# Sample attention of a decoder step: fp32 products replaced by three passes over high and low parts

## The chip, the cores and the metric

The kernel runs on one core of one Trainium2 chip. The metric is the device time of one execution in microseconds (us); lower is better. All times below come from the runs and from one profiled execution of the kernel before.

## The reference

One inference step of a small decoder: a gated convolution layer, a projection to shared keys and values, dilated window attention of 2048 prompt tokens, and the same for 8 samples with one new token each, whose older keys and values lie in a cache. The part around the change is the samples' attention. For each of three head groups (`GROUPS`), each of 8 samples and each of 2 key/value heads, 4 query heads attend to 128 cached keys and to the new one:

```python
def window_attn_sample(q, kc, vc, n_past, window, dilation):
    ...
    s = jnp.einsum('btkgd,btnkd->btkgn', qg, kg) * SCALE
    lse = jax.nn.logsumexp(s, axis=-1)
    p = jnp.exp(s - lse[..., None])
    o = jnp.einsum('btkgn,btnkd->btkgd', p, vg).reshape(Bd, T, HEADS, HEAD_DIM)
    return o, lse.reshape(Bd, T, HEADS)
```

The three groups are then mixed with weights from their softmax denominators. Everything is fp32.

## The kernel before

The program is five phases, one after the other, with a barrier between them: convolution projection (names `a_`), convolution output (`b_`), prompt attention with its projections (`g_`), sample attention (`s_`, `sample_attention_phase`), and the output phase (`d_`). In phases a, b, g and d every large fp32 product is written as three passes: ScalarE (ACT) copies the operand into a tile of type fp32r (the high part), VectorE (DVE) subtracts it from the original (the low part), and TensorE (PE) accumulates high x high, high x low and low x high in PSUM.

The sample phase keeps plain fp32 products. Its engines run orders written out by hand; there is no scheduler, and semaphores alone tie the engines together.

- SyncE (SP) loads six half caches (`s_cache`, two per group), the queries and the new rows, and then the 16 row blocks of the two weight matrices of the output phase, through `RAW` buffers `w_raw`. Block k is issued when the low part of block k - RAW is made.
- TensorE turns the queries (`single("q", g)`), then for each group (`scores(g)`) turns the cached keys in quads of four 128x128 tiles (`turn_keys`, L1625) into two PSUM tiles `tps`, and multiplies each turned key tile with the 4 query columns that belong to it (L1644). A quad is turned while the one before it is still being worked on. Sixteen such products fill one PSUM bank; it is copied, turned back, goes through the softmax, and the probabilities are turned again. `values(g)` multiplies the 16 cached value tiles, straight from `s_cache`, with 4 columns of probabilities each (L1663). The order is: scores 0, scores 1, values 0, scores 2, values 1, values 2.
- ScalarE copies turned keys to SBUF (L1710), copies scores, does the exponentials, and in between makes the high parts of the weight blocks for the output phase (L1703).
- VectorE does the new key's scores, the maxima, the low parts of the weight blocks (L1781, L1784) and the final merge.

In all, L1644 and L1663 each stand for 48 products of a 128x128 stationary tile with 4 moving columns.

Of the kernel before, what the change touches and what calls it, by code (L numbers as in the profile page):

```python
# [14 lines left out]
F32 = mybir.dt.float32  # L15
F32R = mybir.dt.float32r
BF16 = mybir.dt.bfloat16
ALU = mybir.AluOpType
# [1477 lines left out]
def sample_attention_phase(nc, q_sample, new_rows, caches, o_sample, w_z, w_out, pre_gain, w_hi, w_lo):  # L1496
# [10 lines left out]
    with ExitStack() as ctx:  # L1507
        def sb(name, shape, dt=F32):
            return ctx.enter_context(nc.sbuf_tensor(f"s_{name}", shape, dt))
# [8 lines left out]
        cache = [sb(f"cache{c}", [P, NS // 2, 2 * KVW]) for c in range(2 * GROUPS)]  # L1518
        q_rows = sb("q_rows", [R, GROUPS, HD])
        new = sb("new", [R, GROUPS, 2, HD])  # L1520
        qt = [sb(f"qt{g}", [P, R]) for g in each]
        keys_t = [sb(f"keys_t{b}", [P, 4, P]) for b in range(2)]
        score_t = [sb(f"score_t{g}", [P, R]) for g in each]
        score = [sb(f"score{g}", [R, KEYS + 1]) for g in each]
        prob = [sb(f"prob{g}", [R, KEYS + 1]) for g in each]
        prob_t = [sb(f"prob_t{g}", [P, R]) for g in each]
        sum_t = [sb(f"sum_t{g}", [P, R]) for g in each]
        product = sb("product", [R, HD])
        sums = sb("sums", [R, GROUPS, HD])
        stat = sb("stat", [R, 4, GROUPS])  # L1530
        small = sb("small", [R, 4])
        merged = sb("merged", [R, HD])
        ident = sb("ident", [P, P])
        gains = sb("gains", [P, KT])
        RAW = 3
        w_raw = [sb(f"w_raw{b}", [P, D]) for b in range(RAW)]

        tps = [ps(f"tps{b}", [P, 4, P]) for b in range(2)]
# [6 lines left out]
        s_new_rows = sem("new_rows_landed")  # L1545
        s_cache = [sem(f"cache_landed{c}") for c in range(2 * GROUPS)]
        s_keys = sem("keys_turned")
        s_keys_sb = sem("keys_copied")
        s_one = sem("single_turned")
        s_one_sb = sem("single_copied")  # L1550
        s_st = sem("scores_t_ready")
# [57 lines left out]
        @block.tensor  # L1609
        def _(pe):  # L1610
            def single(kind, g, src, rows):

                n = SINGLES.index((kind, g))
                if n >= 2:
                    pe.wait_ge(s_one_sb, n - 1)
                nc.tensor.transpose(one[n % 2][0:src.shape[1], 0:rows], src, ident[0:rows, 0:rows]).then_inc(s_one, 1)

            def turn_keys(g, quad):

                n, c = 4 * g + quad, 2 * g + quad // 2  # L1620
                pe.wait_ge(s_cache[c], 16)
                if n >= 2:
                    pe.wait_ge(s_keys_sb, n - 1)
                for x in range(4):
                    t = nc.tensor.transpose(tps[n % 2][:, x, :],  # L1625
                                            cache[c][:, 2 * (quad % 2) + x // 2, (x % 2) * HD:(x % 2 + 1) * HD],
                                            ident[:])
                t.then_inc(s_keys, 1)

            def scores(g):  # L1630

                turn_keys(g, 0)
                for quad in range(4):
                    n = 4 * g + quad
                    if quad < 3:
                        turn_keys(g, quad + 1)
                    pe.wait_ge(s_keys_sb, n + 1)
                    if quad == 0:
                        pe.wait_ge(s_one_sb, done("q", g))
                        if g >= 2:  # L1640
                            pe.wait_ge(s_st_sb, g - 1)
                    for x in range(4):
                        row = (4 * quad + x) * QPK
                        t = nc.tensor.matmul(st_ps[g % 2][:, row:row + QPK], keys_t[n % 2][:, x, :],  # L1644
                                             qt[g][:, row:row + QPK], start=True, stop=True)
                t.then_inc(s_st, 1)

            def turn_scores(g):
                pe.wait_ge(s_st_sb, g + 1)
                single("score", g, score_t[g][:], P)  # L1650

            def turn_probs(g):
                pe.wait_ge(s_exp, g + 1)
                single("prob", g, prob[g][:, 0:KEYS], R)

            def values(g):

                pe.wait_ge(s_one_sb, done("prob", g))
                if g >= 2:
                    pe.wait_ge(s_ot_sb, g - 1)  # L1660
                for pair in range(NS * KVH):
                    seq, n = pair // KVH, pair % KVH
                    t = nc.tensor.matmul(ot_ps[g % 2][:, pair * QPK:(pair + 1) * QPK],  # L1663
                                         cache[2 * g + seq // 4][:, seq % 4, KVW + n * HD:KVW + (n + 1) * HD],
                                         prob_t[g][:, pair * QPK:(pair + 1) * QPK], start=True, stop=True)
                t.then_inc(s_ot, 1)

            def turn_sums(g):
                pe.wait_ge(s_ot_sb, g + 1)
                single("sum", g, sum_t[g][:], P)  # L1670

            pe.wait_ge(s_ident, 2)
            pe.wait_ge(s_q, 16 * GROUPS)
            for g in each:
                single("q", g, q_rows[:, g, :], R)
            scores(0)
            turn_scores(0)
            scores(1)
            turn_scores(1)
            turn_probs(0)  # L1680
            values(0)
            scores(2)
            turn_scores(2)
            turn_probs(1)
            turn_sums(0)
            values(1)
            turn_probs(2)
            values(2)
            turn_sums(1)
            turn_sums(2)  # L1690

        @block.scalar
        def _(act):
            def copy_single(kind, g, dst):
                act.wait_ge(s_one, done(kind, g))
                act.wait_ge(s_one_sb, done(kind, g) - 1)
                nc.scalar.activation(dst, bank(kind, g)[0:dst.shape[0], 0:dst.shape[1]], ACT.Copy)\
                  .then_inc(s_one_sb, 1)

            def split_weights(ks):  # L1700
                for k in ks:
                    act.wait_ge(s_wraw[k % RAW], 16 * (k // RAW + 1))
                    nc.scalar.activation(w_hi[:, k // KT, k % KT, :], w_raw[k % RAW][:], ACT.Copy,  # L1703
                                         scale=gains[:, k:k + 1] if k < KT else 1.0).then_inc(s_whi, 1)

            def keys(g, weights=()):
                for quad in range(4):
                    n = 4 * g + quad
                    act.wait_ge(s_keys, n + 1)
                    nc.scalar.activation(keys_t[n % 2][:], tps[n % 2][:], ACT.Copy).then_inc(s_keys_sb, 1)  # L1710
                    split_weights(weights[quad:quad + 1])
                act.wait_ge(s_st, g + 1)
                nc.scalar.activation(score_t[g][:], st_ps[g % 2][:, 0:R], ACT.Copy).then_inc(s_st_sb, 1)
                copy_single("score", g, score[g][:, 0:KEYS])

            def exponentials(g):
                act.wait_ge(s_bias, 2 * g + 2)
                nc.scalar.activation(prob[g][:], score[g][:], ACT.Exp, bias=stat[:, 0, g:g + 1], scale=SCALE,
                                     accum_out=stat[:, 1, g:g + 1]).then_inc(s_exp, 1)
                copy_single("prob", g, prob_t[g][:])  # L1720

            def copy_sums(g):
                act.wait_ge(s_ot, g + 1)
                nc.scalar.activation(sum_t[g][:], ot_ps[g % 2][:, 0:R], ACT.Copy).then_inc(s_ot_sb, 1)

            act.dma_start(gains[:], pre_gain.rearrange("(k p) -> p k", p=P),
                          allow_slow_non_contiguous=True).then_inc(s_gains, 16)
            for g in each:
                copy_single("q", g, qt[g][:])
            keys(0)  # L1730
            act.wait_ge(s_gains, 16)
            keys(1, range(0, 4))
            exponentials(0)
            split_weights(range(4, 6))
            copy_sums(0)
            keys(2, range(6, 10))
            exponentials(1)
            split_weights(range(10, 13))
            copy_sums(1)
            exponentials(2)  # L1740
            split_weights(range(13, 16))
            copy_sums(2)
            act.wait_ge(s_step, 3)
            nc.scalar.activation(stat[:, 2, :], stat[:, 3, :], ACT.Exp).then_inc(s_w, 1)

        @block.vector
        def _(dve):
            def new_score(g):

                if g > 0:  # L1750
# [24 lines left out]
            def split_weights(ks):  # L1775

                for k in ks:
# [5 lines left out]
                    else:  # L1783
                        nc.vector.tensor_tensor(lo, w_raw[k % RAW][:], hi, ALU.subtract).then_inc(s_wlo, 1)  # L1784

            dve.wait_ge(s_q, 16 * GROUPS)
            dve.wait_ge(s_new_rows, 16 * GROUPS)
            for g in each:
                new_score(g)
            maximum(0)  # L1790
            dve.wait_ge(s_gains, 16)
            split_weights(range(0, 4))
            maximum(1)
            split_weights(range(4, 10))
            maximum(2)
            add_new_value(0)
            split_weights(range(10, 16))

            least, total, inverse = small[:, 1:2], small[:, 2:3], small[:, 3:4]
            dve.wait_ge(s_bias, 2 * GROUPS)  # L1800
# [482 lines left out]
```

## Time and profile before

| What | Value |
|---|---|
| Time, median of 3 runs (lowest to highest) | 2868.02 us (2867.28 to 2869.19) |
| Span of the profiled execution, first to last instruction | 2864.1 us |
| What lies around the span, by the median | 3.9 us |
| PE busy / PE weight load busy | 2717.9 us (95%) / 2351.9 us (82%) |
| DVE busy / ACT busy | 1189.8 us (42%) / 973.7 us (34%) |
| Sample phase, first instruction to the first one of the output phase | 2361.33 to 2434.63 us: 73.3 us |

The profile gives no execution time of its own for the profiled run beside the span, so the 3.9 us is the median less the span. Each core instruction has a start and a length; a TensorE product shows as a weight load (PEld) and a matmul (PE), whose end is modelled, so the spacing of starts is the better measure of its cost. The granted TensorE clock is given as a share of 2.4 GHz: 1.00 is 2.4 GHz, 0.50 is 1.2 GHz.

### The profile page before, as it was taken

The numbers are of one execution on the slowest core, as the hardware profiler recorded it, in microseconds if no ns is written. First come the engines' busy times: TensorE is split into PE (matmuls) and PEld (weight loads), VectorE is DVE, ScalarE is ACT, GpSimd is POOL, SyncE is SP. The second block draws the span as 40 slices with busy tenths as digits, with TensorE's granted clock in tenths as the row PEclk, the third lists the DMA queues.
The fourth block names the chain that finished last, engine by engine and source line by source line (L and its number), as shares of the span: only waits on it lengthen the run. The fifth ranks groups of instructions, "written<-read, shape, count | busy, mean of one in ns | idle before, by whom it ended". The sixth has DMA issues, their size and how long they took to land. (4 is left out here: it accounts for less than half of the span.)

```text
span 2864.1 us, 39445 instructions
## 1 busy us (share of the span) xinstructions
PE 2717.9 (95%) x14124; PEld 2351.9 (82%) x14124; DVE 1189.8 (42%) x2209; ACT 973.7 (34%) x2163; POOL 449.0 (16%) x330
## 2 busy tenths in 40 slices
PE   6999999999799799999989999989999987899997
PEld 5999999999777568888858888877888867788884
DVE  7311111111243355555564554554444433455552
ACT  6211111111155434444443443343333333233332
POOL 1010110101012211111111111111111110233331
PEclk9999999999999999999999999999999985999999
DMA  4232323322455431111131111131111116433330
GB/s 155 85 103 70 109 95 106 103 70 95 142 189 174 139 130 49 41 40 41 63 104 43 48 48 41 46 120 51 60 59 59 50 37 210 170 133 133 134 119 31
DMA packets 128411, 264.49 MB, mean 92 GB/s; under 512 B 14125, under 2 KB 81541, under 8 KB 126794
## 3 DMA queue, kind: packets, MB, share of 16 engines
q1 hardware_dynamic: 122138, 219.41, 23.3%
q10 hardware_dynamic: 6192, 44.01, 4.8%
q8 instruction: 50, 0.82, 0.1%
q14 instruction: 31, 0.25, 0.0%
HBM read 198.21 MB, written 109.19 MB: 107 GB/s over the span
## 5 line engine op out<-in xcount | busy, mean ns | idle before, releaser
L1070 PE MATMUL g_proj<-g_w_hi,g_ht_hi 128*128 128x512 f32 (+1 forms) x1224 | 509.2, 416 | 19.7 <-DVE g_w_lo L1385 19.4
L1072 PE MATMUL g_proj<-g_w_hi,g_ht_lo 128*128 128x512 f32 (+1 forms) x1224 | 485.5, 397 | 0.0
L1071 PE MATMUL g_proj<-g_w_lo,g_ht_hi 128*128 128x512 f32 (+1 forms) x1224 | 485.1, 396 | 0.0
L249 PE MATMUL a_pair<-a_ht_hi,a_w_hi 128*128 128x412 f32 (+1 forms) x1280 | 448.9, 351 | 2.0 <-DVE a_ht_lo L409 2.0
L251 PE MATMUL a_pair<-a_ht_hi,a_w_lo 128*128 128x412 f32 (+1 forms) x1280 | 448.1, 350 | 0.0
L250 PE MATMUL a_pair<-a_ht_lo,a_w_hi 128*128 128x412 f32 (+1 forms) x1280 | 448.0, 350 | 0.0
L1070 PEld LDWEIGHTS g_proj<-g_w_hi,g_ht_hi 128*128 128x128 f32 (+1 forms) x1224 | 223.5, 183 | 72.9 <-DVE g_w_lo L1385 14.2
L1072 PEld LDWEIGHTS g_proj<-g_w_hi,g_ht_lo 128*128 128x128 f32 (+1 forms) x1224 | 223.1, 182 | 64.1 <-issue 3.2
L1071 PEld LDWEIGHTS g_proj<-g_w_lo,g_ht_hi 128*128 128x128 f32 (+1 forms) x1224 | 224.1, 183 | 49.5 <-issue 2.4
L249 PEld LDWEIGHTS a_pair<-a_ht_hi,a_w_hi 128*128 128x128 f32 x1280 | 241.6, 189 | 3.0 <-DVE a_ht_lo L409 2.4
L250 PEld LDWEIGHTS a_pair<-a_ht_lo,a_w_hi 128*128 128x128 f32 x1280 | 241.4, 189 | 1.0
L251 PEld LDWEIGHTS a_pair<-a_ht_hi,a_w_lo 128*128 128x128 f32 x1280 | 241.3, 188 | 0.6
L1456 POOL TENSOR_TENSOR g_q_rot<-g_rot_a,g_rot_b 128x512 f32<-128x512 f32 (+1 forms) x102 | 131.0, 1286 | 652.4 <-DVE g_rot_b L1355 652.4
L1258 ACT ACTIVATE g_probs<-g_score,g_part 128x256 f32<-128x256 f32 (+1 forms) x384 | 159.6, 428 | 114.5 <-DVE g_part L1379 114.5
L1371 DVE TENSOR_TENSOR g_score<-g_score,g_mask 128x1024 f32<-128x1024 f32 (+1 forms) x96 | 96.8, 1009 | 227.8 <-PE g_score L1103 227.8
L209 POOL TENSOR_TENSOR a_w_lo<-a_w_raw,a_w_hi 128x1024 fp32r<-128x1024 f32 x32 | 76.2, 2406 | 619.5 <-ACT a_w_hi L307 619.5
L1330 DVE TENSOR_TENSOR g_pt_lo<-g_tps,g_pt_hi 128x512 fp32r<-128x512 f32 x152 | 99.8, 687 | 119.5 <-ACT g_pt_hi L1228 119.5
L463 DVE TENSOR_TENSOR a_y<-a_pair,a_conved 128x412 f32<-128x412 f32 (+1 forms) x40 | 23.4, 586 | 293.7 <-ACT a_silu_z L329 293.7
L620 PE MATMUL b_out<-b_w_hi,b_y_hi 128*128 128x512 f32 (+1 forms) x272 | 108.2, 398 | 25.5 <-DVE b_w_lo L706 16.3
L1266 ACT ACTIVATE g_sum_t<-g_out 128x512 f32<-128x512 f32 x96 | 57.4, 598 | 204.2 <-PE g_out L1132 204.2
L427 DVE TENSOR_TENSOR a_u<-a_c,a_pair 128x412 f32<-128x412 f32 (+1 forms) x40 | 23.3, 583 | 232.7 <-ACT a_c L311 232.7
L329 ACT ACTIVATE a_silu_z<-a_pair 128x412 f32<-128x412 f32 (+1 forms) x40 | 20.6, 514 | 288.0 <-PE a_pair L251 288.0
(222 smaller groups left out, 4924.6 us busy)
## 6 DMA issues: line engine op xcount, KB each, us to landing
out_cache_kv_g_sample<-cache_kv_g ACTq DMA_DIRECT2D x72, 410.0 KB, 3.5
scratch_partial<-g_part SPq DMA_DIRECT2D x48, 520.0 KB, 2.9
d_part<-scratch_partial SPq DMA_DIRECT2D x48, 520.0 KB, 4.6
g_tok<-scratch_hn_rows SPq DMA_DIRECT2D x48, 512.0 KB
a_w_raw<-a_w_in SPq DMA_DIRECT2D x32, 512.0 KB, 5.4
a_x<-x_prompt SPq DMA_DIRECT2D x16, 512.0 KB, 3.5
b_y_raw<-scratch_y_t SPq DMA_DIRECT2D x16, 512.0 KB, 4.3
b_x<-x_prompt SPq DMA_DIRECT2D x16, 512.0 KB
```

What stands on the lines that cost most here:

```text
L209: nc.gpsimd.tensor_tensor(w_lo[k][:], w_raw[k % 2][:], w_hi[k][:].bitcast(F32), ALU.subtract).then_inc(s_wlo, 1)
L249: nc.tensor.matmul(out, hi, ht_hi[:, k, cols], start=(k == 0), stop=False)
L250: nc.tensor.matmul(out, hi, ht_lo[:, k, cols], start=False, stop=False)
L251: last = nc.tensor.matmul(out, lo, ht_hi[:, k, cols], start=False, stop=(k == KT - 1))
L620: nc.tensor.matmul(out, hi, w_hi[:, k, cols], start=(k == 0), stop=False)
L1070: nc.tensor.matmul(out, hi, w_hi[:, k, cols], start=(k == 0), stop=False)
L1071: nc.tensor.matmul(out, hi, w_lo[:, k, cols], start=False, stop=False)
L1072: last = nc.tensor.matmul(out, lo, w_hi[:, k, cols], start=False, stop=(k == KT - 1))
L1258: nc.scalar.activation(probs[:, h, cols], score[:, h, cols], ACT.Exp, bias=part[w.u % 2][:, D + x:D + x + 1], scale=SCALE, accum_out=part[ ...
L1330: nc.vector.tensor_tensor(lo, bank_view(at[1], width, hi), hi.bitcast(F32), ALU.subtract).then_inc(s_tr_free, 1)
L1371: nc.vector.tensor_tensor(score[:, :, cols], score[:, :, cols], m.unsqueeze(1).to_broadcast([P, QPK, width]), ALU.add).then_inc(s_masked, 1)
L1456: nc.gpsimd.tensor_tensor(dst[0:n, 0:heads * HD], rot_a[0:n, bank, 0:heads * HD], rot_b[0:n, bank, 0:heads * HD], ALU.add).then_inc(s_rot, 1)
```

## The change

The sample phase gets the three passes too. Turned queries, turned keys, cached values and turned probabilities are each split into a high part (ACT, fp32r) and a low part (DVE), and each fp32 product becomes three accumulating fp32r products. The values, which were used straight from the cache, are now first split into `v_hi` and `v_lo`, one pair of buffers per half cache, used again for each group. The single turned tiles of queries and probabilities are released by DVE's subtraction in place of ACT's copy. In the same diff the weight blocks get two landing buffers where there were three, `merged` shares the memory of `product`, and the program is built with `dynamic_dma_scratch_size=1024`.

```diff
-        qt = [sb(f"qt{g}", [P, R]) for g in each]
-        keys_t = [sb(f"keys_t{b}", [P, 4, P]) for b in range(2)]
+        qt_hi = [sb(f"qt_hi{g}", [P, R], F32R) for g in each]
+        qt_lo = [sb(f"qt_lo{g}", [P, R], F32R) for g in each]
+        keys_hi = [sb(f"keys_hi{b}", [P, 4, P], F32R) for b in range(2)]
+        keys_lo = [sb(f"keys_lo{b}", [P, 4, P], F32R) for b in range(2)]
+        v_hi = [sb(f"v_hi{b}", [P, NS // 2, KVW], F32R) for b in range(2)]
+        v_lo = [sb(f"v_lo{b}", [P, NS // 2, KVW], F32R) for b in range(2)]
...
-        merged = sb("merged", [R, HD])
+        merged = product
...
-        RAW = 3
+        RAW = 2
...
-                        t = nc.tensor.matmul(st_ps[g % 2][:, row:row + QPK], keys_t[n % 2][:, x, :],
-                                             qt[g][:, row:row + QPK], start=True, stop=True)
+                        out, cols = st_ps[g % 2][:, row:row + QPK], slice(row, row + QPK)
+                        nc.tensor.matmul(out, keys_hi[n % 2][:, x, :], qt_hi[g][:, cols], start=True, stop=False)
+                        nc.tensor.matmul(out, keys_hi[n % 2][:, x, :], qt_lo[g][:, cols], start=False, stop=False)
+                        t = nc.tensor.matmul(out, keys_lo[n % 2][:, x, :], qt_hi[g][:, cols], start=False, stop=True)
...
-                    t = nc.tensor.matmul(ot_ps[g % 2][:, pair * QPK:(pair + 1) * QPK],
-                                         cache[2 * g + seq // 4][:, seq % 4, KVW + n * HD:KVW + (n + 1) * HD],
-                                         prob_t[g][:, pair * QPK:(pair + 1) * QPK], start=True, stop=True)
+                    if pair % (NS * KVH // 2) == 0:
+                        pe.wait_ge(s_vlo, 2 * g + seq // 4 + 1)
+                    out, cols = ot_ps[g % 2][:, pair * QPK:(pair + 1) * QPK], slice(pair * QPK, (pair + 1) * QPK)
+                    hi, lo = (v[seq // 4][:, seq % 4, n * HD:(n + 1) * HD] for v in (v_hi, v_lo))
+                    nc.tensor.matmul(out, hi, prob_hi[g][:, cols], start=True, stop=False)
+                    nc.tensor.matmul(out, hi, prob_lo[g][:, cols], start=False, stop=False)
+                    t = nc.tensor.matmul(out, lo, prob_hi[g][:, cols], start=False, stop=True)
...
+            def values_high(g):
+                for half in range(2):
+                    act.wait_ge(s_cache[2 * g + half], 16)
+                    if g > 0:
+                        act.wait_ge(s_ot, g)
+                    nc.scalar.activation(v_hi[half][:], cache[2 * g + half][:, :, KVW:2 * KVW], ACT.Copy).then_inc(s_vhi, 1)
...
-                    nc.scalar.activation(keys_t[n % 2][:], tps[n % 2][:], ACT.Copy).then_inc(s_keys_sb, 1)
+                    if n >= 8:
+                        act.wait_ge(s_st, n // 4 - 1)
+                    nc.scalar.activation(keys_hi[n % 2][:], tps[n % 2][:], ACT.Copy).then_inc(s_keys_hi, 1)
...
             keys(0)
             act.wait_ge(s_gains, 16)
+            values_high(0)
             keys(1, range(0, 4))
             exponentials(0)
             split_weights(range(4, 6))
             copy_sums(0)
+            values_high(1)
             keys(2, range(6, 10))
             exponentials(1)
             split_weights(range(10, 13))
             copy_sums(1)
+            values_high(2)
             exponentials(2)
...
+            def single_low(kind, g, hi, lo):
+                dve.wait_ge(s_one_hi, [x for x in SINGLES if x[0] in ("q", "prob")].index((kind, g)) + 1)
+                dve.wait_ge(s_one_sb, done(kind, g) - 1)
+                nc.vector.tensor_tensor(lo, bank(kind, g)[0:P, 0:R], hi.bitcast(F32), ALU.subtract).then_inc(s_one_sb, 1)
+
+            def keys_low(g, weights=()):
+                for quad in range(4):
+                    n = 4 * g + quad
+                    dve.wait_ge(s_keys_hi, n + 1)
+                    nc.vector.tensor_tensor(keys_lo[n % 2][:], tps[n % 2][:], keys_hi[n % 2][:].bitcast(F32),
+                                            ALU.subtract).then_inc(s_keys_sb, 1)
+                    split_weights(weights[quad:quad + 1])
+
+            def values_low(g):
+                for half in range(2):
+                    dve.wait_ge(s_vhi, 2 * g + half + 1)
+                    nc.vector.tensor_tensor(v_lo[half][:], cache[2 * g + half][:, :, KVW:2 * KVW],
+                                            v_hi[half][:].bitcast(F32), ALU.subtract).then_inc(s_vlo, 1)
...
+            for g in each:
+                single_low("q", g, qt_hi[g][:], qt_lo[g][:])
+            keys_low(0)
...
             maximum(0)
             dve.wait_ge(s_gains, 16)
-            split_weights(range(0, 4))
+            values_low(0)
+            keys_low(1, range(0, 4))
             maximum(1)
-            split_weights(range(4, 10))
+            single_low("prob", 0, prob_hi[0][:], prob_lo[0][:])
+            split_weights(range(4, 6))
+            values_low(1)
+            keys_low(2, range(6, 10))
             maximum(2)
+            single_low("prob", 1, prob_hi[1][:], prob_lo[1][:])
             add_new_value(0)
-            split_weights(range(10, 16))
+            split_weights(range(10, 13))
+            values_low(2)
+            single_low("prob", 2, prob_hi[2][:], prob_lo[2][:])
+            split_weights(range(13, 16))
...
-    nc = bacc.Bacc("TRN2", target_bir_lowering=False, num_devices=1)
+    nc = bacc.Bacc("TRN2", target_bir_lowering=False, num_devices=1, dynamic_dma_scratch_size=1024)
```

## Rows read from the trace of the kernel before

**Rows 1.** Profile page, part 2: granted TensorE clock in 40 slices of 71.6 us.
```profile
PEclk9999999999999999999999999999999985999999
```

**Rows 2.** Busy time of stretches: length, engines with instruction counts, granted clock, DMA share, GB/s.
```profile
2394.20:2401.00 6.80, 6.80 (x32) 6.80 (x33) 2.48 (x2) 1.99 (x2) 0.00 (x0) 0.50 0.69 214
...
2413.40:2420.40 7.00, 7.00 (x33) 6.90 (x32) 3.85 (x4) 2.93 (x3) 0.00 (x0) 0.50 0.64 212
2420.40:2428.60 8.20, 7.19 (x34) 6.98 (x34) 3.94 (x6) 3.66 (x7) 0.00 (x0) 0.50 0.12 49
...
2442.00:2447.30 5.30, 5.24 (x12) 4.13 (x13) 2.34 (x8) 1.51 (x2) 3.21 (x2) 0.50 0.97 382
```

**Rows 3.** Groups of the sample phase by shape: busy us, mean ns | idle before.
```profile
L1644 PEld LDWEIGHTS s_scores_t<-s_qt,s_keys_t 128*128 128x128 f32 x96 | 21.4, 331 | 2.3 <-ACT s_keys_t L1710 2.3
L1644 PE MATMUL s_scores_t<-s_qt,s_keys_t 128*128 128x4 f32 x96 | 21.1, 348 | 1.2 <-ACT s_keys_t L1710 1.2
L1663 PE MATMUL s_sums_t<-s_prob_t,s_cache 128*128 128x4 f32 x96 | 21.0, 355 | 0.6 <-ACT s_prob_t L1697 0.6
...
L1625 PE MATMUL s_tps<-s_ident,s_cache 128*128 128x128 f32 x48 | 12.4, 427 | 0.0
...
L1784 DVE TENSOR_TENSOR w_output_lo<-s_w_raw,w_output_hi 128x1024 fp32r<-128x1024 f32 x8 | 9.5, 1223 | 7.1 <-ACT w_output_hi L1703 7.1
...
L1703 ACT ACTIVATE w_output_hi<-s_w_raw 128x1024 fp32r<-128x1024 f32 x8 | 8.1, 1048 | 0.3 <-DMA s_w_raw<-b_w_out 0.3
```

**Rows 4.** Timeline, prompt phase's last tile: start us, length us, fp32r products and a load.
```profile
2344.19 0.41 PE L1102 MATMUL g_score<-g_kt_lo,g_qt_hi 128*128 128x128 f32 x1
...
2346.32 0.41 PE L1103 MATMUL g_score<-g_kt_hi,g_qt_lo 128*128 128x128 f32 x1
...
2353.20 0.33 PEld L1131 LDWEIGHTS g_out<-g_pt_hi,g_v_lo 128*128 128x128 f32 x1
```

**Rows 5.** Weight loads of the whole kernel by shape.
```profile
L250 PEld LDWEIGHTS a_pair<-a_ht_lo,a_w_hi 128*128 128x128 f32 x1280 | 241.4, 189 | 1.0
...
L1101 PEld LDWEIGHTS g_score<-g_kt_hi,g_qt_hi 128*128 128x128 f32 x384 | 74.0, 193 | 8.9 <-DVE g_kt_lo L1330 3.5 <-issue 3.2
L1055 PEld LDWEIGHTS g_tps<-g_ident,g_probs 128*128 128x128 f32 x608 | 70.2, 141 | 6.6 <-issue 0.2
```

**Rows 6.** Timeline of the output phase's start: a high part, its low part, the first product.
```profile
2440.68 0.60 ACT L2043 ACTIVATE d_ht_hi<-d_tps 128x512 fp32r<-128x512 f32 x1 [0.26 <-PE d_tps L1980]
2441.31 0.69 DVE L2099 TENSOR_TENSOR d_ht_lo<-d_tps,d_ht_hi 128x512 fp32r<-128x512 f32 x1 [0.16 <-ACT d_ht_hi L2043]
2442.06 0.29 PEld L2000 LDWEIGHTS d_z<-w_output_hi,d_ht_hi 128*128 128x128 f32 x1 [1.81 <-DVE d_ht_lo L2099]
```

**Rows 7.** Timeline of the sample phase, ACT and PE around each block of products.
```profile
2371.19 1.87 PE L1644 MATMUL s_scores_t<-s_qt,s_keys_t 128*128 128x4 f32 x8
...
2380.44 0.27 ACT L1697 ACTIVATE s_score<-s_one 64x128 f32<-64x128 f32 x1 [0.51 <-PE s_one L1616]
...
2382.00 1.87 PE L1644 MATMUL s_scores_t<-s_qt,s_keys_t 128*128 128x4 f32 x8
...
2385.98 1.87 PE L1644 MATMUL s_scores_t<-s_qt,s_keys_t 128*128 128x4 f32 x8 [1.16 <-ACT s_keys_t L1710]
...
2401.20 0.23 ACT L1724 ACTIVATE s_sum_t<-s_sums_t 128x64 f32<-128x64 f32 x1 [5.01 <-PE s_sums_t L1663]
...
2402.80 1.87 PE L1644 MATMUL s_scores_t<-s_qt,s_keys_t 128*128 128x4 f32 x8
...
2420.46 0.22 ACT L1724 ACTIVATE s_sum_t<-s_sums_t 128x64 f32<-128x64 f32 x1 [3.85 <-PE s_sums_t L1663]
...
2421.80 6.99 PE L1663 MATMUL s_sums_t<-s_prob_t,s_cache 128*128 128x4 f32 x32 [0.31 <-ACT s_prob_t L1697]
```

**Rows 8.** DVE reading a smaller PSUM tile, same timeline, prompt phase's end.
```profile
2355.99 0.42 DVE L1336 COPY g_part<-g_tps 128x256 f32<-128x256 f32 x1 [3.01 <-ACT g_part L1233]
```

**Rows 9.** The weight blocks' loads (tile `s_w_raw`), issue to landing.
```profile
DMA to landing us min/median/max: 3.4/4.4/13.9
```

More of the change, by code:

```diff
@@ L1525, in sample_attention_phase @@
         prob = [sb(f"prob{g}", [R, KEYS + 1]) for g in each]
-        prob_t = [sb(f"prob_t{g}", [P, R]) for g in each]
+        prob_hi = [sb(f"prob_hi{g}", [P, R], F32R) for g in each]
+        prob_lo = [sb(f"prob_lo{g}", [P, R], F32R) for g in each]
         sum_t = [sb(f"sum_t{g}", [P, R]) for g in each]
@@ L1547, in sample_attention_phase @@
         s_keys = sem("keys_turned")
-        s_keys_sb = sem("keys_copied")
+        s_keys_hi = sem("keys_hi_ready")
+        s_keys_sb = sem("keys_lo_ready")
+        s_vhi = sem("values_hi_ready")
+        s_vlo = sem("values_lo_ready")
+        s_one_hi = sem("single_hi_ready")
         s_one = sem("single_turned")
@@ L1696, in copy_single @@
                 act.wait_ge(s_one_sb, done(kind, g) - 1)
-                nc.scalar.activation(dst, bank(kind, g)[0:dst.shape[0], 0:dst.shape[1]], ACT.Copy)\
-                  .then_inc(s_one_sb, 1)
+                t = nc.scalar.activation(dst, bank(kind, g)[0:dst.shape[0], 0:dst.shape[1]], ACT.Copy)
+                t.then_inc(s_one_sb if kind == "score" else s_one_hi, 1)
+            def values_high(g):
[4 more added lines that the diff above has]
+                    nc.scalar.activation(v_hi[half][:], cache[2 * g + half][:, :, KVW:2 * KVW], ACT.Copy).then_inc(s_vhi, 1)
             def split_weights(ks):
@@ L1719, in exponentials @@
                                      accum_out=stat[:, 1, g:g + 1]).then_inc(s_exp, 1)
-                copy_single("prob", g, prob_t[g][:])
+                copy_single("prob", g, prob_hi[g][:])
             def copy_sums(g):
@@ L1728, in _ @@
             for g in each:
-                copy_single("q", g, qt[g][:])
+                copy_single("q", g, qt_hi[g][:])
             keys(0)
             act.wait_ge(s_gains, 16)
+            values_high(0)
             keys(1, range(0, 4))
```

## Prediction

> **What bounds the kernel now.** I read the page first: PE is busy nearly throughout at a full clock, and only two slices of the clock row fall, an 8 and a 5 [rows 1]. They cover the end of the prompt phase and the sample phase, which is all that the diff touches, so the question is what 73.3 us out of 2864.1 become. Second, the stretches of that phase: in two of them PE is busy all of the time (6.80 of 6.80 us, 7.00 of 7.00), and the granted clock is 0.50, the 1.2 GHz level, in all of them; it is still 0.50 in the first 5.3 us of dense 512-column products of the next phase [rows 2]. Third, the groups by shape: 96 records for 48 score products and 96 for 48 value products, so an fp32 product with 4 columns is two matmuls and two loads of 128x128 weights; PE's idle time ahead of these groups is 1.2 and 0.6 us [rows 3]. So PE sets the length of the phase: ACT and DVE mostly wait for it, and the next phase starts behind a barrier that the phase's end opens. What is added to PE's time here is added to the kernel's time; what is added on ACT and DVE counts where PE waits for it.
>
> **The passes.** 32 records start in a stretch of 6.80 us: 0.213 us each [rows 2]. Their length is a load's length, not that of 4 columns: loads show 0.331 us each and overlap [rows 3]. The change makes 48 fp32r records of a block of 16 products where 32 stood. The sample phase has no fp32r product, so the price comes from the prompt phase's end: at 1.2 GHz ten steps of fp32r score products with 128 columns take 2344.19 to 2346.32, again 0.213 us each, and an fp32r load there shows 0.33 us, as the fp32 load does [rows 4]. 128 columns alone can't explain that: the next phase's 512-column products go at 12 in 5.24 us [rows 2], so columns stream at about 0.85 ns each, 0.11 us for 128. The load sets it, and with 4 columns it will too. Two passes with the same stationary tile don't save a load: the second pass over the same high part in the convolution phase has all of its 1280 loads [rows 5]. Bounds for one pass: 0.213 us from above; from below, a load as cheap as a transposition's, which shows 141 against 193 ns at the full clock [rows 5], 52 ns less, or 0.104 us at half of it, which leaves 0.109 us. I take 0.213, since the load of this very type at this very clock was seen. Six blocks x 16 more records x 0.213 = **+20.4 us**.
>
> The Trainium skill, "TensorE: Matmul & The Clock Gate", section "LDWEIGHTS (loading the stationary operand)", has a load take its columns divided by 1.2, in ns, with no word of the data type: an estimate of 107 ns for 128 columns. By that the 288 passes would take 30.8 us and the term would be about -10 us; the rows at 0.213 us speak against it.
>
> **Start of the phase.** The first high part of keys was followed by PE at once; now a low part stands between. In the output phase that step exists: high part 0.60 us, low part 0.69 us, product 0.78 us after the high part's end [rows 6]. The first score product, at 2371.19 before [rows 7], comes 0.7 us later. The three query tiles are now released by DVE's subtraction of a 128x64 PSUM tile: 0.42 us for 256 columns [rows 8] and 0.69 for 512 [rows 6] give about 0.22 for 64. The third query waits for the first low part, 0.3 us more, and the keys are turned behind it. Together **+1.0**. Inside a block the low parts cost nothing: a quad is now 12 products, 2.6 us, and its cover is the quad before it; a high and a low part (1.3 us) and one weight block on ACT (1.05) and on DVE (1.22) [rows 3] fit into it and the 0.9 us in which the next quad is turned. Without that cover each quad would cost 0.7.
>
> **The split of the values.** It stands in ACT's and DVE's order at three places, and each time PE has nothing else queued that it may do. A high part of half a cache is 128x1024 on ACT, 1.05 us; a low part on DVE is 1.22 us [rows 3]. The next operation starts about 0.1 us ahead of the end that ACT shows.
> - Before scores 1: ACT's score copy starts at 2380.44 and the first product followed at 2382.00, 1.56 later [rows 7]. Now: 0.17 to the first high part, 1.05, 0.1 to DVE, two low parts 2.44, the key's low part 0.69 behind them on DVE, 0.06 to PE: 4.4 with the overlaps (the key's high part, third on ACT, is ready by 2.65). **+2.85**.
> - Before scores 2: from copy_sums(0) at 2401.20 to the product at 2402.80 it was 1.60 [rows 7]; now the same chain, 4.4: **+2.8**.
> - Before values 2: from copy_sums(1) at 2420.46 to the product at 2421.80 it was 1.34 [rows 7]. Now 0.12 + 1.05 + 0.1 + 2.44, then the low part of the probabilities 0.22 and 0.06: 4.0. The exponential, behind both high parts on ACT, gives its own high part by 3.2 and is not the last. **+2.6**.
> - Before values 0 and 1 only the probabilities' low part is new, 0.3 each: **+0.6**.
>
> **What goes away.** PE idled 1.16 us before the second quad of scores 1 [rows 7], because ACT stood at the first weight block, not yet landed. PE now reaches that point some 8 us later, when the block is there: **-1.2**.
>
> **Edits at nothing.** `merged` in place of `product`: its first writer is long done. The smaller scratch: the kernel issues no DMA from POOL. The waits on `s_st` and `s_ot` ask for what ACT's order already implies. Two weight buffers: a block is issued when the low part two before it is made, and takes 4.4 us to land by the median [rows 9]. In scores 1 block 2 is issued 1.2 us after quad 4 starts and lands at 5.6; its high part ends at 6.65, its low part at 7.95, the key's low part behind it on DVE at 8.65. PE wants that at 9.5 (2.6 + 0.9 + 2.6 + 0.9 + 2.6). So 0.8 us is left; scores 2 has the same pattern.
>
> **Sum.** 20.4 + 1.0 + 2.85 + 2.8 + 2.6 + 0.6 - 1.2 = 29.05. The span of 2864.1 becomes 2893.2; with the 3.9 us around it, which makes up the median of 2868.0, that is **2897 us**, 1.0% slower.
>
> **Rivals.**
> - *The clock rises in the sample phase* (not slower). Blocks of 48 records run 10 us without a gap, which PE had not done here before. At 2.4 GHz a pass takes half of 0.213: 288 x 0.107 = 30.8 against 192 x 0.213 = 40.9, so -10.1, with the waits of +8.65 (29.05 less 20.4) -1.5. The 48 turned tiles (12.4 us by their lengths [rows 3]) would give back some 5 more and the next phase's 5.3 slow us [rows 2] half of themselves: down to -9; I take -7, 2861 us. It decides from a mean pass of (40.9 - 8.65) / 288 = 0.112 us. Against it: stretches with PE busy for all of 6.8 and 7.0 us stood at 0.50 from end to end [rows 2], and the new records are the same loads with 4 columns. The Trainium skill, in the same page's "Why this matters for your kernels", advises to keep TensorE continuously busy for the full throughput, by which these blocks would speed up; the rows so far don't bear that out for products this thin. Chance 5%.
> - *The fp32r load is cheap* (no change): passes at 0.109 us give 288 x 0.109 - 40.9 = -9.5, with the waits -0.85: 2867 us. Against it both rows at 0.213 and the loads at 0.33 [rows 4]. It is also what the skill's load rule gives. Chance 3%.
> - *The two landing buffers bind* (slower still): from a landing of 5.2 us on, DVE's low part of quads 7 and 11 is late by the excess. Loads took from 3.4 up to 13.9 us, though the longest stood behind the half caches, which are done by then [rows 9]. At 8 us it costs 3 us twice: 2903. Chance 6%.
>
> **How the numbers follow.** My forecast has 86%. Its own spread is 2893 to 2901: the serial chains may overlap more than I let them (1 us each), or handoffs may cost more. The range of 2891 to 2902 adds the lower part of the third rival and some room below; it leaves out the first two (8%), the upper part of the third (4%) and the tails. A measurement of this kernel tells about 0.2%, 5.7 us, from no change. Slower by more: the forecast and the third rival, 92%. Same: the cheap load and the upper edge of the clock rival, 4%. Faster: the rest of the clock rival, 4%.
>
> **What would show it.** L1644 and L1663 give way to three lines each with 48 records, 288 in all, starting every 0.213 us at a clock of 0.50. PE waits 2.9 us for DVE's key low part at the first quad of scores 1 and of scores 2, and some 3.9 us between values 1 and values 2. The phase lasts 102 us where it lasted 73. A clock of 1.00 in the phase, passes near 0.11 us, or PE waiting inside scores 1 and 2 would make this wrong.

## The result, and the profile after

The changed kernel takes **2895.2 us** (median of 4 runs, 2894.0 to 2897.1) where the kernel before takes 2867.9: a ratio of 1.0097, 95% interval 1.0084 to 1.0110. It is 27.3 us slower; the forecast was 2897. The profiled execution took 2894.0 us, its span is 2892.0 us against 2864.1. Of the runs below, one of the version with all value splits under cover took 13874 us and is left out of its figure.

The page's clock row after, beside [rows 1]: the low slices read 6, 5 and 8 where they read 8 and 5. The phase that runs at the low clock is longer; a part of the difference comes from the slices' edges, which lie later because the slices are longer (that of the 6 ends 25 us into the sample phase, that of the 8 before the change ended 1.5 us into it).

```profile
PEclk9999999999899899999999999999999965899999
```

One stretch of scores 0, with the columns of [rows 2]: 45 records in 9.40 us, PE busy for 9.36 of them, and the granted clock is 0.50, the 1.2 GHz level.

```profile
2374.00:2383.40 9.40, 9.36 (x45) 9.27 (x45) 2.17 (x8) 1.20 (x3) 0.00 (x0) 0.50 1.05 392
```

The groups by shape, which answer to [rows 3]: three lines of 48 records where L1644 and L1663 had 96, and a load of 128x128 for every one of them, as long as the fp32 load was (0.331 us).

```profile
L1654 PE MATMUL s_scores_t<-s_qt_hi,s_keys_hi 128*128 128x4 f32 x48 | 17.0, 354 | 5.6 <-DVE s_keys_lo L1784 5.6
L1679 PE MATMUL s_sums_t<-s_prob_lo,s_v_hi 128*128 128x4 f32 x48 | 16.9, 353 | 0.0
...
L1655 PEld LDWEIGHTS s_scores_t<-s_qt_lo,s_keys_hi 128*128 128x128 f32 x48 | 16.0, 333 | 0.0
```

PE's three largest waits in the phase (in total, times, longest), without those for a DMA at its start:

```profile
PE s_scores_t L1654 <- DVE s_keys_lo L1784: 5.6, 3, 2.7
PE s_one L1625 <- ACT s_prob L1742: 4.1, 3, 2.6
PE s_sums_t L1678 <- DVE s_prob_lo L1778: 1.6, 3, 0.8
```

The timeline, which answers to [rows 7]. The first and the last line are the same step of two phases' starts, so their distance is the length of the sample phase: 101.8 us (before: 2361.33 to 2434.63, 73.3 us). Between them stand the chain from the score copy to scores 1, the first and last product of values 1, and the chain from values 1 to values 2.

```profile
2360.50 0.20 POOL L1613 MEMSET s_ident<- 128x128 f32 x1 [21.77 <-POOLq L2270]
...
2384.13 0.27 ACT L1712 ACTIVATE s_score<-s_one 64x128 f32<-64x128 f32 x1 [0.51 <-PE s_one L1625]
2384.30 1.99 ACT L1720 ACTIVATE s_v_hi<-s_cache 128x1024 fp32r<-128x1024 f32 x2
...
2385.45 2.36 DVE L1791 TENSOR_TENSOR s_v_lo<-s_cache,s_v_hi 128x1024 fp32r<-128x1024 f32 x2 [0.49 <-ACT s_v_hi L1720]
...
2387.73 0.68 DVE L1784 TENSOR_TENSOR s_keys_lo<-s_tps,s_keys_hi 128x512 fp32r<-128x512 f32 x1
...
2388.47 0.37 PE L1654 MATMUL s_scores_t<-s_qt_hi,s_keys_hi 128*128 128x4 f32 x1 [2.67 <-DVE s_keys_lo L1784]
...
2431.82 0.37 PE L1678 MATMUL s_sums_t<-s_prob_hi,s_v_hi 128*128 128x4 f32 x1 [0.22 <-DVE s_prob_lo L1778]
...
2441.87 0.35 PE L1680 MATMUL s_sums_t<-s_prob_hi,s_v_lo 128*128 128x4 f32 x1
2442.26 0.22 ACT L1748 ACTIVATE s_sum_t<-s_sums_t 128x64 f32<-128x64 f32 x1 [3.85 <-PE s_sums_t L1680]
...
2444.81 0.37 PE L1625 MATMUL s_one<-s_ident,s_prob 64*128 64x64 f32 x1 [2.58 <-ACT s_prob L1742]
...
2446.01 0.37 PE L1678 MATMUL s_sums_t<-s_prob_hi,s_v_hi 128*128 128x4 f32 x1 [0.84 <-DVE s_prob_lo L1778]
2446.25 0.35 PE L1679 MATMUL s_sums_t<-s_prob_lo,s_v_hi 128*128 128x4 f32 x1
2446.46 0.35 PE L1680 MATMUL s_sums_t<-s_prob_hi,s_v_lo 128*128 128x4 f32 x1
2446.67 0.35 PE L1678 MATMUL s_sums_t<-s_prob_hi,s_v_hi 128*128 128x4 f32 x1
2446.89 0.35 PE L1679 MATMUL s_sums_t<-s_prob_lo,s_v_hi 128*128 128x4 f32 x1
2462.27 0.20 POOL L2250 MEMSET d_ident<- 128x128 f32 x1 [101.13 <-POOLq L2279]
```

Read from the bottom: passes start every 0.21 us. Values 1 takes 10.40 us from its first start to its last end. Values 2 begins 3.75 us after the copy of the sums at 2442.26; PE idles there first for the exponential, which stands on ACT behind two high parts of values (2.58 us), then for the low part of the probabilities. Scores 1 begins 4.34 us after the score copy at 2384.13: two high parts, two low parts, and only then the key's low part. For values 1 the kernel before has one line:

```profile
2413.44 6.99 PE L1663 MATMUL s_sums_t<-s_prob_t,s_cache 128*128 128x4 f32 x32
```

### The profile page after: what moved, and what is told of

Its sections match the earlier page's. It is cut to its first block and busy times, and to the rows that moved or that the text cites. A ratio compares the mean times of both kernels' runs of the same rounds, so it can differ in the third digit from the quotient of the medians.

```text
span 2892.0 us, 39683 instructions
## 1 busy us (share of the span) xinstructions
PE 2739.2 (95%) x14220; PEld 2372.9 (82%) x14220; DVE 1209.1 (42%) x2233; ACT 979.3 (34%) x2169; POOL 447.9 (15%) x330
```

## The experiments

Each ran beside the kernel before on the same chip. The "phase" is always the distance of the two lines above, in one profiled execution. It is the better measure of a few microseconds: in these profiles the phase begins anywhere from 2359.8 to 2367.8 us, though nothing ahead of it was changed. In the cuts of code, "..." stands for lines left out.

**One pass fewer.** The product with the low part of queries and of probabilities is left out, so part of the sums is missing.

```
-  nc.tensor.matmul(out, keys_hi[n % 2][:, x, :], qt_lo[g][:, cols], start=False, stop=False)
...
-  nc.tensor.matmul(out, hi, prob_lo[g][:, cols], start=False, stop=False)
```

> Leaves out one of the three passes of both products (high part of the keys or values with the low part of the queries or probabilities); all splits on ScalarE and VectorE stay. Theory (each pass is one load of 128x128 weights at 0.213 us on the path): 96 records fewer, 20.4 us less than the changed kernel, about 2875 us. Rival (the added time comes from the splits and their waits, with the third pass in their shadow): less than 5 us gained, 2890 us or more.

Measured: 2879.8 us, 1.0045 (1.0028 to 1.0061); the phase 84.7 us, 17.1 less than after. Each value block lost 3.41 us for 16 records, 0.213 each, so the 96 records are 20.4 us. Of these 2.3 came back as a longer wait, and 0.6 behind PE's last product of the phase:

```profile
PE s_scores_t L1654 <- DVE s_keys_lo L1782: 7.9, 5, 2.7
```

In the changed kernel this wait is 5.6 in 3. With only 8 passes in a quad the cover is thinner, and ACT stands for weight blocks that haven't landed (4.0 us in 3 times for `b_w_in` and 10.0 in 6 for `b_w_out`; in the changed kernel 0.7 in 1 and 8.9 in 3), with the key's high part behind them. So a pass costs what the prediction has it cost, and the weight blocks are the next thing to bind, one pass away.

**Thin stationary tiles.** In the second and third pass the operands change places: 4 columns of queries or probabilities are loaded, the 128 columns of keys or values stream. Their results go to a spare corner of the bank, so the sum of the three parts is left out.

```
...
-  nc.tensor.matmul(out, keys_hi[n % 2][:, x, :], qt_lo[g][:, cols], start=False, stop=False)
-  t = nc.tensor.matmul(out, keys_lo[n % 2][:, x, :], qt_hi[g][:, cols], start=False, stop=True)
+  turned = st_ps[g % 2][0:QPK, 2 * P:3 * P]
+  nc.tensor.matmul(turned, qt_lo[g][:, cols], keys_hi[n % 2][:, x, :], start=True, stop=True)
+  t = nc.tensor.matmul(turned, qt_hi[g][:, cols], keys_lo[n % 2][:, x, :], start=True, stop=True)
...
```

> Same count of passes, but the second and the third of each product have their operands swapped: the 4 columns of queries or probabilities are stationary and the 128x128 tile streams; their result goes to an unread corner of the bank, so the output lacks these two terms. Theory (the load of 128 columns sets 0.213 us): a swapped pass is set by 128 streamed columns, 0.107 us at 1.2 GHz, 192 x 0.106 = 20.4 us less, about 2875 us. Rival (0.213 us is a floor of an fp32r pass of up to 128 columns, whichever operand is loaded): no change, 2895 us.

Measured: 2876.9 us, 1.0039 (1.0025 to 1.0053), the phase 82.7 us. Three products of a pair now take 0.35 us at the low clock (2382.87 to 2383.22, granted clock 0.50), not 0.64:

```profile
2382.87 0.31 PE L1654 MATMUL s_scores_t<-s_qt_hi,s_keys_hi 128*128 128x4 f32 x1
2383.05 0.27 PE L1656 MATMUL s_scores_t<-s_keys_hi,s_qt_lo 128*4 128x128 f32 x1
2383.11 0.31 PE L1657 MATMUL s_scores_t<-s_keys_lo,s_qt_hi 128*4 128x128 f32 x1
2383.22 0.31 PE L1654 MATMUL s_scores_t<-s_qt_hi,s_keys_hi 128*128 128x4 f32 x1
```

The pass's price is the wide load, not a floor under every product. The expectation had the clock at its low level throughout; it was at 1.00 from 2374.6 to 2381.4 and from 2412.1 to 2415.5, as the column shows:

```profile
2376.00:2380.00 4.00, 2.18 (x21) 1.75 (x21) 2.17 (x10) 2.09 (x4) 0.00 (x0) 1.00 1.06 388
...
2412.00:2416.00 4.00, 1.78 (x22) 1.59 (x21) 1.97 (x3) 2.60 (x3) 0.00 (x0) 0.93 0.50 143
```

In these two times 13 of the 96 pairs ran; the comparison of 0.35 with 0.64 doesn't need them. The 28 us that 96 pairs save at the low clock (0.29 each) shortened the phase by 19.0 only: PE's wait for the keys' low parts went from 5.6 to 14.0 us, while ACT's wait for the weight blocks of `b_w_in` went from 0.7 to 8.3. That the total came near what was expected is partly that cancellation.

**Value splits under cover.** Those of groups 0 and 1 are made behind the second and the third quad of scores 0 and of scores 2, a half each (`values=` in the diff; DVE's order is changed likewise), not between the blocks. Nothing is left out.

```
-  keys(0)
+  keys(0, values=0)
...
-  values_high(0)
...
-  values_high(1)
-  keys(2, range(6, 10))
+  keys(2, range(6, 10), values=1)
```

> The splits of the values of groups 0 and 1 are moved: each half stands behind the second and third quad of keys of scores 0 and scores 2 in ScalarE's and VectorE's order, where TensorE is busy, no longer ahead of scores 1 and 2. Theory (these splits cost only where TensorE waits for them): the two waits of 2.8 and 2.6 us go, 5.4 us less, about 2890 us. Rival (ScalarE and VectorE have no room inside a block, so the wait only moves to a later quad): within 1.5 us of the changed kernel.

Measured: 2891.3 us, 1.0087 (1.0070 to 1.0105), the phase 98.0 us: 3.8 less, not 5.4.

```profile
PE s_scores_t L1654 <- DVE s_keys_lo L1784: 1.8, 3, 0.7
```

A wait of up to 0.7 stays: the first quad's own low part, which nothing covers either. Of the 2.78 and 2.61 us that the two gaps grew by, the value split is 1.9 each, and most of the rest is that low part.

**A raised clock at the start.** Fifteen 512-column products on a constant tile fill PE's wait for the queries.

```
+  for _ in range(15):
+      nc.tensor.matmul(ot_ps[1][:], keys_hi[0][:, 0, :], keys_hi[0][:].rearrange("p a b -> p (a b)"),
+                       start=True, stop=True)
```

> Adds 15 products of 512 fp32r columns on TensorE at the start of the phase, where it waits 7 us for the queries; nothing reads their result. Theory (thin passes do not hold the higher clock): the clock may rise for a moment, and falls back to 0.50 in the first blocks: 0 to 5 us less than the changed kernel, 2890 to 2896 us. Rival (the clock is low only because the phase begins idle, and TensorE without gaps keeps it up): passes at 0.107 us, the phase some 30 us shorter, about 2865 us.

Measured: 2895.1 us, 1.0101 (1.0084 to 1.0118). In the stretches the clock column reads 0.94 and 0.91 after the filler and 0.50 from 2376 on, in a stretch in which PE is busy for 4.00 of 4.00 us with the change's products:

```profile
2368.00:2372.00 4.00, 3.13 (x17) 2.09 (x15) 0.67 (x3) 1.08 (x4) 0.00 (x0) 0.94 1.09 319
2372.00:2376.00 4.00, 3.04 (x25) 3.04 (x25) 1.64 (x3) 1.27 (x3) 0.00 (x0) 0.91 1.06 320
2376.00:2380.00 4.00, 4.00 (x21) 4.00 (x21) 1.67 (x7) 0.60 (x1) 0.00 (x0) 0.50 1.05 387
```

The clock rises, and these products don't keep it. The wait of 1.0 us that PE has ahead of them (2371.99 to 2372.97) need not be the reason: in the restaged version below PE idles for 1.6 us (2377.34 to 2378.90) in a stretch whose clock reads 1.00. The phase is 99.0 us, 2.8 less than after, most of it in scores 0, which takes 9.9 us and not 11.9; the total doesn't show it.

**Three landing buffers.** The split values are written over the cache tiles, and the room goes to a third landing buffer. The order is that of the change; one wait is added, for the turning of the keys in the tile that is written over, and the order already implies it. Nothing is left out.

```
-  RAW = 2
+  RAW = 3
...
```

> The changed kernel with three landing buffers for the weight blocks in place of two; the high and low parts of the values are written over the memory of the cache tiles to make room, in the same order and behind the same waits as in the changed kernel. Everything of the reference is computed. If the two landing buffers hold nothing up in the changed kernel (theory): 2895, within 1.5 us, the sample phase 101 to 102 us, TensorE's waits for the low parts of the keys still 5 to 6 us in three. If they are what spaces the last weight blocks and the splits between them (rival): 2890 or less.

Measured: 2897.9 us, 1.0107 (1.0091 to 1.0124), the phase 101.7 us, and PE's wait for the low parts is the same:

```profile
PE s_scores_t L1657 <- DVE s_keys_lo L1788: 5.7, 3, 2.7
```

ACT's 8.9 us of waiting for `b_w_out` are gone, and that buys nothing: they were off the path.

**All value splits under cover.** As in the third experiment, and group 2's split behind the exponentials of group 1, written over its own cache tiles.

```
   exponentials(1)
+  values_high(2)
   split_weights(range(10, 13))
...
-  values_high(2)
   exponentials(2)
```

> The changed kernel with every value split moved under work of TensorE: those of groups 0 and 1 behind the second and third quad of keys, that of group 2 behind the exponentials of group 1, written over the cache tiles' memory so that it waits for no earlier products. Everything of the reference is computed. Theory (three gaps of 2.85, 2.8 and 2.6 us each hold a value split, of which about 0.65 is the first quad's own low part): 2895.2 less 3.8 (measured for the first two) less 2.2 is 2889, the pause between values 1 and values 2 falling from 3.75 to about 1.6 us. What is left over the kernel before is then the passes' 20.4. Rival (the pause before values 2 is set by the turning of the probabilities and not by the value split): 2891, as with the first two alone.

Measured: 2889.1 us (2888.1 to 2893.6), 1.0075 (1.0055 to 1.0095). By the total it can't be told from the third experiment (2889.5 to 2892.8); by the trace the phase is 96.5 us, 5.2 less than after and 1.5 less than there. Values 2 begins 1.6 us after the copy of the sums, as expected, so that gap gave 2.2; a new wait of 0.7 inside scores 0 took a part back. The exponential is no longer late:

```profile
PE s_scores_t L1657 <- DVE s_keys_lo L1786: 2.5, 4, 0.7
PE s_one L1628 <- ACT s_prob L1746: 2.2, 3, 0.7
PE s_sums_t L1681 <- DVE s_prob_lo L1780: 1.4, 3, 0.6
```

What is left over the kernel before, 23 us of phase, is mainly the passes and the first low parts.

**Operands swapped throughout.** Queries and probabilities are loaded, spread into zeroed tiles of 64 columns of which a pair fills four; keys and values stream; all 48 products of a block add into one 64x128 bank, so that scores and sums come out as rows and need no turning. The value splits are under cover, and the weight blocks have three landing buffers. The cut shows the edit against the changed kernel.

```
-  nc.tensor.matmul(out, keys_hi[n % 2][:, x, :], qt_hi[g][:, cols], start=True, stop=False)
+  q_hi, q_lo = (tile[:, pair * R:(pair + 1) * R] for tile in wide[0])
+  nc.tensor.matmul(out, q_hi, keys_hi[n % 2][:, x, :], start=(pair == 0), stop=False)
+  nc.tensor.matmul(out, q_lo, keys_hi[n % 2][:, x, :], start=False, stop=False)
+  t = nc.tensor.matmul(out, q_hi, keys_lo[n % 2][:, x, :], start=False, stop=(pair == PAIRS - 1))
...
```

> A version of the change with the operands' places swapped: queries and probabilities are the loaded operand, spread into zeroed tiles of 64 columns of which four hold a sample's pair, keys and values stream as 128 columns, and all 48 products of a group add into one bank, so that scores and sums come out in rows and are not turned. Everything of the reference is computed, and by the same three parts. Theory (a step takes the longer of the next operand's load and this one's stream, and 128 columns at the low clock are at most 0.107 us): 288 x 0.107 = 31 us of passes against 61 in the changed kernel and 41 in the kernel before; with the value splits under cover and the turned scores and sums gone the sample phase takes 60 to 64 us, 2855 to 2862. Rival 1 (an fp32r load costs its 0.213 whatever its width): passes 61 as in the changed kernel, some 2885. Rival 2 (ScalarE, VectorE or the weight blocks between the splits become the bound): passes fall as by the theory, but waits for the low parts of the keys of over 8 us in all, 2864 to 2872.

Measured: 2866.8 us, 0.9995 (0.9985 to 1.0004): no difference from before, by the second rival. The phase is 72.4 us. PE is busy for only 30.6 of them, at a granted clock that reads 0.98 and 1.00 from 2380 to 2388 and 1.00 from 2404 to 2424, which the expectation hadn't counted on. It waits 13.6 us for the keys' low parts, 6.9 at once. ACT stands at the first weight block, with the keys behind it (first row), and at the end eight blocks are left that come one by one through three buffers (ACT waits 8.4 us for them):

```profile
2391.87 1.15 ACT L1730 ACTIVATE w_output_hi<-s_w_raw,s_gains 128x1024 fp32r<-128x1024 f32 x1 [5.32 <-DMA s_w_raw<-b_w_in]
2392.93 0.58 ACT L1735 ACTIVATE s_keys_hi<-s_tps 128x512 fp32r<-128x512 f32 x1
...
2423.05 1.06 ACT L1730 ACTIVATE w_output_hi<-s_w_raw 128x1024 fp32r<-128x1024 f32 x1 [3.46 <-DMA s_w_raw<-b_w_out]
2426.21 1.06 ACT L1730 ACTIVATE w_output_hi<-s_w_raw 128x1024 fp32r<-128x1024 f32 x1 [2.10 <-DMA s_w_raw<-b_w_out]
```

**The same, with the weight blocks staged anew.** No block is split before scores 1 is through, and four landing buffers more lie in the first two cache tiles once values 0 is through. The two edits were made together, so what each is worth isn't shown.

```
-  RAW = 3
+  OWN, RAW = 3, 7
+  w_raw += [cache[c][:].rearrange("p s c -> p (s c)")[:, i * D:(i + 1) * D] for c in range(2) for i in range(2)]
...
+  elif k >= OWN:
+      sp.wait_ge(s_ot, 1)
...
```

> The version with swapped operands and spread queries, reordered: no weight block is split before the scores of group 1 are through (the first block landed at 2391.9 in the version before it, 24 us after the phase's start, and ScalarE stood in front of it for 5.3 us with the keys behind it), and four more landing buffers in the first two cache tiles once the values of group 0 are through, in place of three in all. Everything of the reference is computed. Theory (the products are off the path; what ends the phase is the weight blocks, 16 from 2391.9 on at some 1.4 to 1.8 us each, then 6 us of tail): the phase takes 52 to 58 us against 73 in the kernel before and 102 in the changed one, 2848 to 2855. Rival (the landing and not the order held the blocks): still 2860 or more.

Measured: **2851.4 us**, 0.9945 (0.9932 to 0.9959): 16 us faster than before, 44 faster than the change. The phase is 55.9 us. PE is through by 2404; DVE (third of the busy times), busy for 4.00 and 3.96 us of two stretches of 4, is still at the weight blocks and, after the merge, ends the phase with the last four of them at 2416:

```profile
2396.00:2400.00 4.00, 3.23 (x48) 2.91 (x47) 3.43 (x6) 4.00 (x7) 0.00 (x0) 1.00 1.01 409
2400.00:2404.00 4.00, 2.70 (x45) 2.56 (x43) 4.00 (x4) 4.00 (x5) 0.00 (x0) 1.00 0.64 182
2404.00:2408.00 4.00, 0.00 (x0) 0.00 (x0) 3.96 (x6) 1.19 (x2) 0.00 (x0) 0.82 0.92 283
```

**The same with fp32 products.** No high and low parts of queries, keys, values and probabilities: one fp32 product a pair, in the swapped layout and with the same staging.

```
-  nc.tensor.matmul(out, q_hi, keys_hi[n % 2][:, x, :], start=(pair == 0), stop=False)
...
+  t = nc.tensor.matmul(st_ps[g % 2][0:R, 0:P], wide[0][:, pair * R:(pair + 1) * R],
+                       turned[n % 2][:, x, :], start=(pair == 0), stop=(pair == PAIRS - 1))
```

> The version above with fp32 products as in the kernel before in place of the three passes: no high and low parts of queries, keys, values and probabilities, one fp32 product for each sample's pair, operands swapped and spread and weight blocks staged in the same way. Everything of the reference is computed. If the gain of the swapped versions is in layout and staging and not in the passes: within 3 us of the version above, since the weight blocks end the phase in both. If the three passes are what pays once their loads are thin: 5 us or more slower than the version above.

Measured: **2850.2 us**, 0.9935 (0.9922 to 0.9949), the phase 53.9 us. It equals the three-pass version within the intervals, and DVE is busy for 24.0 us of the phase where it was for 39.8. In both, the four added buffers open when values 0 is through, 26.6 and 26.5 us into the phase, and DVE's last weight blocks end it. So the gain over the kernel before lies in layout and staging; the three passes add nothing to it. How much of the layout's part is the raised clock isn't separated. The staging alone wasn't tried on the kernel before; there PE waited for 1.2 and 0.6 us only ahead of its products [rows 3], which leaves it little to gain.

## Why the prediction was right, step by step

- **Passes, +20.4.** Right. Three score and value blocks that nothing else changed (scores 0 and 2, values 1) grew by 3.45, 3.45 and 3.41 us for 16 records more: 0.213 to 0.216 each. All six blocks together grew by 19.1; less the vanished wait below, 19.2 was predicted. One pass fewer takes 0.213 a record off again, and a thin load makes the pass cheap: the load is what is paid. The Trainium skill, "TensorE: Matmul & The Clock Gate", section "LDWEIGHTS (loading the stationary operand)", would load 128 columns in 107 ns, by an estimate from its rule; the 288 passes at 0.213 us don't agree with it.
- **Start, +1.0.** Measured from PE's first operation to the first score product: 2.75 before, 3.73 after, +0.98.
- **Values before scores 1, scores 2 and values 2, +2.85, +2.8, +2.6.** Measured +2.78, +2.61, +2.41. The places and the sums are right. The heading was too simple: up to 0.7 of each of the first two is the key's own low part, as the third experiment showed. The prediction's chain holds it with 0.69, but reading the whole term as the value split put that experiment's expectation 1.6 us too low. In the last gap the exponential was late too, earlier than the low parts by little.
- **Low parts of the probabilities, +0.6.** Measured +0.27 and +0.26.
- **The wait that goes away, -1.2.** Scores 1 grew by 1.92 where scores 0 grew by 3.45: -1.5.
- **Sum.** 0.98 + 19.06 + 7.80 + 0.53 = 28.4, and the phase grew by 28.5, where 29.05 was predicted. Before the phase the run was 0.8 us shorter, after it 0.2 longer: 27.9 in the span. The 3.9 us that the prediction put around the span were not all of that kind: in the runs whose time and span are both on record they differ by 2.0 or less, so the rest was most likely the profiled execution before being faster than the median.
- **The clock rival** falls: 0.50 through the whole phase, and in the fourth experiment a raised clock was not kept. The Trainium skill, "TensorE: Matmul & The Clock Gate", section "Why this matters for your kernels", advises to keep TensorE busy without a break for the full throughput; here it was busy for 9.36 of 9.40 us at 0.50, so this trace doesn't agree.
- **The cheap fp32r load** falls by the pace of 0.213.
- **The landing buffers** didn't bind (the fifth experiment), though the weight blocks were the next thing to: with one pass fewer PE's wait behind them grew by 2.3 us, and staging them anew, in landing and order, took the swapped version from 72.4 to 55.9.

The shared memory of `merged` and the smaller scratch, both put at nothing, weren't run apart; the terms above leave 0.1 us of the phase for them.

Still open: whether a version of the change in which DVE has less to do would fall below the fp32 products. POOL is busy for 6 us of the restaged version's phase and might split some of the weight blocks; that wasn't tried.

## What to carry to other kernels

When a product streams few columns against a wide stationary tile, count loads and not multiply passes: more passes of another type cost more there (61 us for 288, where 192 took 41), and swapping the operands took the three products of a pair from 0.64 to 0.35 us at the same clock. Price a split by who stands behind it in its engine's order, and give each a block of products as cover. When the products get cheap, look at once for what they were hiding; here it was the weight blocks' landing and splitting, which turned a saving on TensorE into nothing until they were staged anew.

## What was not expected of the hardware

- In these traces a step of PE takes about the longer of a load and a stream, not their sum. At a granted clock of 0.50, a step with 128 columns loaded takes 0.213 us whether 4 columns stream (the change) or 128 (the prompt phase, [rows 4]). With 64 columns loaded and 128 streamed, fp32r passes start every 0.107 us at 0.50 and every 0.06 at 1.00, in the restaged version:

```profile
2371.23 0.31 PE L1678 MATMUL s_scores_t<-s_keys_hi,s_wide_hi 128*64 128x128 f32 x1
2371.34 0.31 PE L1679 MATMUL s_scores_t<-s_keys_hi,s_wide_lo 128*64 128x128 f32 x1
2371.44 0.31 PE L1680 MATMUL s_scores_t<-s_keys_lo,s_wide_hi 128*64 128x128 f32 x1
...
2380.49 0.22 PE L1678 MATMUL s_scores_t<-s_keys_hi,s_wide_hi 128*64 128x128 f32 x1
2380.55 0.22 PE L1679 MATMUL s_scores_t<-s_keys_hi,s_wide_lo 128*64 128x128 f32 x1
2380.61 0.22 PE L1680 MATMUL s_scores_t<-s_keys_lo,s_wide_hi 128*64 128x128 f32 x1
```

- An fp32 product in that layout is two records too, and at a granted clock of 1.00 they start about every 0.11 us: eight in 1.04 us, of which the last shows some 0.27 (an estimate from this row).

```profile
2390.17 1.04 PE L1681 MATMUL s_sums_t<-s_cache,s_wide 128*64 128x128 f32 x8
```

- In the restaged version the granted clock was 1.00 in every stretch of 4 us between 2376 and 2404, with PE busy for 2.4 to 3.7 us of each; in the changed kernel it was 0.50 with PE busy nearly throughout. What of the activity makes the difference was not taken apart.
